# Every second chunk of a gated recurrence mirrored, so that one product serves two chunks on a level, with four level buffers and another order of VectorE's and ScalarE's steps

## The reference

```
x += 0.5 * swiglu(rmsnorm(x))                      # D_FF = 2816
p  = rmsnorm(x) @ w_in ; q,f,i,g | B,C,u = split(p)
     f = lb + (1-lb)*sigmoid(f); k = 1-f           # 4 heads, state 128x128
     S_t = diag(f_t) S_(t-1) + k_t v_t^T ; o_t = S_t^T q_t
     o_hg = rmsnorm(o) * silu(g) ; o_cv = rmsnorm(B * dwconv3(C*u))
x += concat(o_hg, o_cv) @ w_out
x += cross_attention(rmsnorm(x), rmsnorm(mem))     # 256 memory tokens
x += 0.5 * swiglu(rmsnorm(x)) ; return rmsnorm(x)
```

## Time and profile before

| | |
|---|---|
| median of three runs | 1117.04 us |
| the profiled execution | 1116.83 us |
| its span, first to last instruction | 1115.0 us |
| granted TensorE clock, mean over the span | 0.998 |
| TensorE busy | 1103.8 us, 99% of the span |
| VectorE, ScalarE, GpSimd busy | 631.6, 527.8, 439.2 us |

### The profile page before, as it was taken

The page is one execution under the profiler, slowest core; times in us unless marked ns, Lnnn a source line. Parts: engine busy times, 40 slices in busy tenths (PEclk is TensorE's granted clock), DMA queues, the critical chain, the costliest instruction groups (busy, mean ns, idle before and its releaser), DMA issues.

```text
span 1115.0 us, 17502 instructions
## 1 busy us (share of the span) xinstructions
PE 1103.8 (99%) x6434; PEld 971.7 (87%) x6434; DVE 631.6 (57%) x923; ACT 527.8 (47%) x735; POOL 439.2 (39%) x546
## 2 busy tenths in 40 slices
PE   9999999999999999999999999999999999999997
PEld 7889999988888888888888888888899999988886
DVE  7887777442222668888668123466977777430012
ACT  6555555542323555654466443354555555542231
POOL 0000000486665544434548883163000000485651
PEclk9999999999999999999999999999999999999999
DMA  7287675332333221222313442122676665333312
GB/s 240 78 226 185 181 198 169 114 113 95 113 97 110 76 77 57 76 76 76 112 58 127 161 166 76 39 76 75 179 200 179 173 193 169 115 113 99 109 57 76
DMA packets 49458, 136.89 MB, mean 123 GB/s; under 512 B 4736, under 2 KB 11008, under 8 KB 49280
## 3 DMA queue, kind: packets, MB, share of 16 engines
q1 hardware_dynamic: 43888, 118.90, 31.2%
q0 software_dynamic: 4320, 15.73, 8.5%
q10 hardware_dynamic: 1200, 1.57, 0.4%
HBM read 134.09 MB, written 2.10 MB: 122 GB/s over the span
## 4 chain that ended last, share of the span: by engine, by line
PE 53%; POOL 25%; issue 21%; DVE 0%; POOLq 0%; DMA 0%; ACT 0%; DVEq 0%; SPq 0%; ACTq 0%
POOL wl L438 25%; PE bank L1463 8%; PE bank L1465 8%; PE bank L1464 8%; PE bank L1567 4%; PE bank L1569 4%; PE bank L1568 4%; PE score L1567 3%; PE score L1569 3%; PE score L1568 3%; PE o_bank L1567 1%; PE o_bank L1569 1%; PE o_bank L1568 1%; PE bank L1524 1%; PE bank L1528 0%
## 5 line engine op out<-in xcount | busy, mean ns | idle before, releaser
L438 POOL TENSOR_TENSOR wl<-raw,wh 128x256 fp32r<-128x256 f32 x512 | 412.9, 840 | 325.5 <-ACT wh L472 281.2
L472 ACT ACTIVATE wh<-raw 128x1024 fp32r<-128x1024 f32 x120 | 126.0, 1054 | 148.6 <-PE bank L1465 146.4
L1463 PE MATMUL bank<-xh,wh 128*128 128x512 f32 x456 | 182.3, 400 | 0.0
L1465 PE MATMUL bank<-xh,wl 128*128 128x512 f32 x456 | 177.8, 390 | 0.0
L1464 PE MATMUL bank<-xl,wh 128*128 128x512 f32 x456 | 177.5, 389 | 0.0
L452 POOL DMA_DIRECT2D raw<-w_all x30 | 26.1, 869 | 325.1 <-DMA raw<-w_all 325.1
L1463 PE MATMUL bank<-zr,wh 128*128 128x512 f32 (+1 forms) x374 | 142.5, 381 | 0.0
L1465 PE MATMUL bank<-zr,wl 128*128 128x512 f32 (+1 forms) x374 | 141.6, 379 | 0.0
L1464 PE MATMUL bank<-zr,wh 128*128 128x512 f32 (+1 forms) x374 | 140.4, 375 | 0.0
L916 DVE SCALAR_TENSOR_TENSOR x<-bank,x 128x512 f32<-128x512 f32 (+1 forms) x31 | 21.3, 686 | 175.8 <-PE bank L1465 175.8
L1464 PEld LDWEIGHTS bank<-xl,wh 128*128 128x128 f32 x456 | 85.7, 188 | 18.7 <-issue 1.7
(11 more groups left out here) (304 smaller groups left out, 2582.0 us busy)
## 6 DMA issues: line engine op xcount, KB each, us to landing
raw<-w_all SPq DMA_DIRECT2D x200, 512.0 KB, 3.3
raw<-w_all POOLq DMA_DIRECT2D x30, 512.0 KB, 5.4
zf<-w_all SPq DMA_DIRECT2D x30, 256.0 KB, 4.6
x<-x_t SPq DMA_DIRECT2D x8, 256.0 KB, 6.4
out_t<-x SPq DMA_DIRECT2D x8, 256.0 KB, 2.4
raw<-w_all SPq DMA_DIRECT2D x6, 256.0 KB, 6.2
memf<-mem_t ACTq DMA_DIRECT2D x1, 1024.0 KB, 4.8
raw<-w_all ACTq DMA_DIRECT2D x2, 256.0 KB, 4.8
```

Source lines behind the costliest of these rows:

```text
L438: ins = nc.gpsimd.tensor_tensor(wl[:, slot, two], raw[:, slot, two], wh[:, slot, two].bitcast(f32), SUB)
L472: nc.scalar.activation(wh[:, slot, :], raw[:, slot, :], ACT.Copy).then_inc(hi_ready, 1)
L1463: nc.tensor.matmul(out_, a[0], b_[0], start=first, stop=False)
L1465: return nc.tensor.matmul(out_, a[1], b_[0], start=False, stop=last)
```

## The change

Of each pair of chunks the first is now stored mirrored in time. Its keys then lie in the half of a block where the second chunk has its queries, and the other way round. The keys of both fill one stationary tile of 128 columns, and the queries of both one moving tile of 128, so that a level takes two matmuls of 128 columns instead of four of 64. What comes out is one 128 x 128 tile for each pair, its lower triangle for one chunk and its upper for the other; it is collected in `tri` and laid out into `attn` once a head with a second predicated copy. The values of chunks 0 and 2 are mirrored by two matmuls with an exchange matrix (`turn_v`), and the masks for the mirrored chunks are made once, on VectorE under the first down projection (`make_masks`) and with two matmuls. What moves between the two orders of time (q, f, the norm) is written in two halves of 256. Levels rotate through four buffers; `lf` and `convC` get other places. On VectorE the differences of levels 0 and 1 now stand in step A, those of 2 and 3 in L0, and so on, and the factors of a level stand ahead of the differences in L1 and L2; factors of level 6 go to K. On ScalarE the exponentials go one step earlier.

```diff
 def differences(h, a):                       # VectorE
-    if a == 6 or a < 2:
-        if h:
-            dve.wait_ge(score_done, score_no(h - 1, 6 if a == 6 else 4 + a) + 1)
-    else:
-        dve.wait_ge(score_done, score_no(h, a - 2) + 1)
+    if a >= 4:
+        dve.wait_ge(score_done, score_no(h, a - 4) + 1)
+    elif h:
+        dve.wait_ge(score_done, score_no(h - 1, 3 if a == 3 else 4 + a) + 1)
...
 def take_scores(h, a):
-    V_.copy_predicated(at_, mk, sc).then_inc(score_read, 1)
+    V_.copy_predicated(tri[:, :, :], mk, sc).then_inc(score_read, 1)
...
+    V_.copy_predicated(attn[:, :, :].rearrange("p (g c) n -> p g c n", g=2), mk, both_ways)\
+        .then_inc(attn_ready, 1)
...
 def step(kind, h, a):
     if kind == "A":
-        link(V_.tensor_tensor_scan(b[:, :], restart[:, :], lf, 0.0, MULT, ADD))
+        link(V_.tensor_tensor_scan(b[:, :], restart[:, :], lf[:, :], 0.0, MULT, ADD))
-        if h == 0:
-            differences(h, 0)
-            differences(h, 1)
+        differences(h, 0)
+        differences(h, 1)
+    if kind == "L" and a == 0:
+        differences(h, 2)
+        differences(h, 3)
+        dve.wait_ge(k_ready, h + 1)
+        dve.wait_ge(silu_done, SN["q", h] + 1)
+        factors(h, 0)
+        factors(h, 1)
+    if kind == "L" and a == 1:
+        factors(h, 2)
+        factors(h, 3)
+        differences(h, 4)
+        differences(h, 5)
+        take_scores(h, 0)
+        take_scores(h, 1)
+    if kind == "L" and a == 2:
+        factors(h, 4)
+        factors(h, 5)
+        differences(h, 6)
+        V_.tensor_tensor(eb_kd, last.to_broadcast([128, 2, 2, 128]), b_in, SUB).then_inc(diff_ready, 1)
+        take_scores(h, 2)
+        take_scores(h, 3)
     if kind == "K":
+        factors(h, 6)
         take_scores(h, 4)
         take_scores(h, 5)
...
 def step(kind, h, a):                        # ScalarE
-    if kind == "L" and (h, a) != (0, 0):
-        decays(h, a)
+    if kind == "L":
+        if (h, a) != (0, 0) and a == 0:
+            decays(h, 0)
+        decays(h, a + 1)
...
 def step(kind, h, a):                        # TensorE
-    for t in range(TT):
-        last = nc.tensor.matmul(score_bank[s % 2][:, width * t:width * (t + 1)],
-                                lhs[:, 128 * t:128 * t + 128], rhs[:, t], start=True, stop=True)
+    for g in range(2):
+        last = nc.tensor.matmul(sc[:, 128 * g:128 * g + 128], keys_of(l, g), queries_of(l, g),
+                                start=True, stop=True)
...
+def queries_of(a, g):
+    m, first = LEVELS[a], X[:, XW * x_slot(a) + 256 * g:XW * x_slot(a) + 256 * g + 1]
+    return bass.AP(first.tensor, first.offset, [list(first.ap[0]), [2 * m, 64 // m], [256 + m, 2], [1, m]])
...
+def turn_v(t):
+    if t == 0:
+        pe.wait_ge(group_read, G_V + TT + 4)
+    else:
+        pe.wait_ge(v_ready, 1)
+    nc.tensor.matmul(o_bank[:, :], swap.bitcast(f32), V[:, t, :], start=True, stop=True).then_inc(v_turned, 1)
```

More of the change, by code:

```diff
@@ L40 @@
 MASK_COLS = 64 * len(LEVELS) + 128
+PAIR = 258
+XW = T + 128
 U_FFN1 = 0
@@ L917, in update_x, with make_masks @@
                                         op0=MULT, op1=ADD).then_inc(group_read, 1)
+            def make_masks():
+                same = masks[:, 64 * len(LEVELS):]
+                dve.wait_ge(hid_lo, FC)
+                V_.memset(upper, 0.0)
+                link(V_.memset(lower.bitcast(f32), 0.0))
+                V_.tensor_copy(mirrored(swap), same)
+                for a, m in enumerate(LEVELS):
+                    mk = masks[:, 64 * a:64 * a + 64].rearrange("p (n m) -> p n m", m=m)
+                    up_, lo_ = (t_[:, 128 * a:128 * a + 128].rearrange("p (n s m) -> p n s m", s=2, m=m)
+                                for t_ in (upper, lower))
+                    V_.tensor_copy(up_[:, :, 1, :], mk)
+                    lo_ = lo_[:, :, 0, :]
+                    (part, (sn, n), (sm, _)) = [list(d) for d in lo_.ap]
+                    ins = V_.tensor_copy(bass.AP(lo_.tensor, lo_.offset + sn * (n - 1) + sm * (m - 1),
+                                                 [part, [-sn, n], [-sm, m]]), mk)
+                ins.then_inc(masks_in, 1)
+                dve.wait_ge(masks_in, 1)
+                total = gbuf[:, 1, T - 128:]
+                link(V_.tensor_tensor(total, upper[:, 0:128], upper[:, 128:256], ADD))
+                for a in range(2, len(LEVELS)):
+                    link(V_.tensor_tensor(total, total, upper[:, 128 * a:128 * a + 128], ADD))
+                V_.tensor_copy(triangles[:, 1, :], total)
+                link(V_.tensor_tensor(total, total, same, ADD))
+                link(V_.tensor_scalar(triangles[:, 0, :], total, -1.0, 1.0, MULT, ADD))
             def ffn(norm, which):
@@ L1155, in ffn @@
                 if which == 0:
+                    make_masks()
                     with dve.Fori(0, KC // 4) as i:
@@ L1280, in step @@
+                    V_.tensor_tensor(kd, kd, f_of(h), MULT).then_inc(kd_ready, 1)
                 if kind == "Q":
@@ L1303, in step @@
                     dve.wait_ge(rms_ready, R["N", h] + 1)
-                    V_.tensor_tensor(onrm, o_bank[:, :], osq[:, :], MULT).then_inc(o_read, 1)
+                    for c in range(2):
+                        out_ = by_chunk(onrm)[:, :, c, :]
+                        last = V_.tensor_tensor(out_ if c else mirrored(out_), by_chunk(o_bank[:, :])[:, :, c, :],
+                                                by_chunk(osq[:, :])[:, :, c, :], MULT)
+                    last.then_inc(o_read, 1)
                     dve.wait_ge(o_read, h + 1)
```

225 lines of the change are left out of this document (141 added, 84 removed).

## The result

The changed kernel takes 1134.37 us (median of four runs, 1132.64 to 1135.59) against 1116.67 for the kernel before, run four times beside it: a ratio of 1.0153, interval 1.0134 to 1.0173. The forecast of 1123.2 had the sign and most places of the stalls; the loss is 17.7 us where it had 6.4.

What follows compares the result with a forecast made beforehand. TensorE bounds the kernel now, with VectorE nearly level and setting the end of the recurrence after the change. 2.9 + 3.45 = 6.35 us on the profiled 1116.83 gave 1123.2 us; 8-in-10 range 1108.5 to 1127.

Steps and rivals of the forecast that it cites:

- TensorE: what goes: Score levels on TensorE: 0.38 us saved for each of 28 levels, 10.6 us in all.
- The rival of 128 being as dear as four 64: Score matmuls: two of 128 columns cost as much as four of 64, nothing saved, 1124 to 1127; chance 0.02.
- The rival of the slowly read moving tile: Queries at m = 1 and 2: alternating columns double the records' cost, 3.7 us over 8 levels, 1125 to 1127; chance 0.05.
- What comes: Added TensorE work: 1.8 us for turning the values and 0.4 for mask matmuls, 2.2 us in sum.
- Hidden work: make_masks, 8.5 us under VectorE's 12.45 us wait at the first down product, and mixer-start clearings: no cost.
- A new wait, head 0: Before head 0's first scores: TensorE stalls 3.4 us for factors behind added differences; head 1's query moves by +2.9 us.
- The stretch to the last key product: Head 1's query to head 3's last key product: VectorE's chain grows from 115.1 to 119.6 us and sets the end.
- the three waits that were to go: VectorE's waits in that stretch for kd (1.9 us), X (1.4) and scores (0.3) vanish: -3.6 us.
- The norm's idleness: VectorE before onrm in three norms: 2.4 us idle each instead of 1.7 in all, +5.5 us.
- Behind that point TensorE's work is the same: After head 3's last key product: TensorE's work unchanged and VectorE has idle time, so no difference.
- 1.05 us of slack: Between the end of head 3's last key product and TensorE's use of it: 1.05 us, subtracted from the chain's growth.
- TensorE stays the bound: Recurrence: VectorE's idle time absorbs the additions, TensorE's waits stay under 5 us; 1109.1 us, from 1105.7 to 1114; chance 0.33.

Runs made afterwards that it cites:

- g2: e7 with take_scores of levels 0 to 3 also moved ahead of the differences in L1 and L2: 1111.71 us (0.9955 to the kernel before).
- f4: Changed kernel's mirroring and four buffers, with VectorE's and ScalarE's steps in the old order and the mask tables at SBUF's far end: 1118.00 us (1.0007).
- e7: e1 plus head 0-1-level factors ahead of the differences of levels 2 and 3 in L0, and g4's norm edit: 1114.90 us (0.9983).
- h2: Kernel before with four unused VectorE differences of 256 columns ahead of head 0's first factors, to make TensorE stall: 1123.81 us (1.0054).
- g4: e1 with the norm's table load, Ln and Exp ahead of the slot's decays on ScalarE: 1118.88 us (1.0023).
- e1: Changed kernel with only its two new mask tables, levels and triangles, moved to the far end of SBUF: 1128.01 us (1.0094).
- e2: Kernel before with an unused tensor of 1152 bytes a partition ahead of the hidden tiles: 1121.34 us (1.0041).
- f1: Kernel before with its seven small tensors at the far end of SBUF, so later tensors begin at a multiple of 2048 bytes: 1119.51 us (1.0024).

## Why the prediction was wrong

Two terms failed. TensorE's work outside the change was put at no difference, and it took 4.9 us more. And a stall was taken to cost its length, where the clock that fell behind it added to the price. Without the 4.9 us the time would still be 1129.5, above the range. In the order of the prediction:

**"TensorE: what goes": 10.6 us.** About right. The kernel before first, then the changed one; a pair of levels lasts from its start to that of the next product:

```profile
377.60 1.89 PE L1703 MATMUL score<-X 128*128 128x64 f32 x16
379.30 0.48 PE L1463 MATMUL bank<-wh,xh 128*128 128x512 f32 x1
```

```profile
392.48 1.06 PE L1832 MATMUL score<-X 128*128 128x128 f32 x8
393.29 0.48 PE L1589 MATMUL bank<-wh,xh 128*128 128x512 f32 x1
...
406.31 0.82 PE L1832 MATMUL score<-X 128*128 128x128 f32 x4
406.96 1.06 PE L1836 MATMUL score<-qf 128*128 128x128 f32 x8
407.86 0.60 PE L1847 MATMUL n_bank<-ident,both 128*128 128x128 f32 x4
```

1.70 became 0.81 for a pair, and 0.84 became 0.65 for level 6. With some 0.87 for the pair of levels 4 and 5 (0.83 where nothing delays it, in g2) that is 2.8 in a head and 11.4 us in four. As the kernels run, short delays inside the groups take some of it back: f4, e7 and g2 keep 8.2 to 8.8 us. The term did not decide the forecast, since the sum went by VectorE's chain. The rival of 128 being as dear as four 64 falls.

The rival of the slowly read moving tile was right in kind and small in size. The four records of level 6 (m = 1) take 0.65 us, the eight of the diagonal, of the same shape but with queries that lie side by side, 0.90. The single records start 112 ns apart for m of 4 and more, 120 to 124 for m = 2 and 165 for m = 1; the keys are read side by side at every level. In the kernel before, all levels have 112. That is 0.2 us a head for level 6 and 0.04 for level 5, 1.0 us in all, where the rival had 3.7. What comes was right (0.85 for turning the values, 405.46 to 406.31).

**"Hidden work": nothing.** Right, but barely. `make_masks` took from 235.52 to 248.15, 12.6 us where I had 8.5, since its conversions of 64 columns from uint8 took 0.75 each while GpSimd worked and 0.18 without it. What is left of the 12.45 us of wait:

```profile
248.50 0.69 DVE L986 SCALAR_TENSOR_TENSOR x<-bank,x 128x512 f32 x1 [0.34 <-DVE triangles L1013]
```

**"A new wait, head 0": +2.9 with a stall of 3.4.** The last factor was forecast for 381.8; it ends at 383.51, and 2.4 of that came from ahead of the mixer. The stall is 1.66 and 1.02. So the mechanism is right and the size nearly (2.7 us for 3.4), and the step failed at its price: a stall was taken to cost its length. The stretch lost 5.2 us. From the first product behind the scores to the next scores it is 8.04 us (384.44 to 392.48) and was 5.56 (379.30 to 384.86): twelve products begun at half the clock, 2.5 us. h2, where nothing else is changed, loses 5.6 us at such a stall, of which 2.7 are the clock's.

**"The stretch to the last key product": 119.6 us, +4.5.** In the prediction's marks (414.86, where head 1's query is read, to 537.20, the end of the key product) it is 122.3 us, 2.7 too many; the table's marks give +7.0. VectorE is busy 99.6 us instead of 97.0, the 2.6 that the copy and the halves were put at, and the three waits that were to go are gone. The norm's idleness is 8.4 us instead of 1.7, so +6.7 where I had +5.5; by head 2.5 to 3.0. It is also the term that g4 takes away. The second predicated copy cost 0.80 us, as its row said:

```profile
L1346 DVE COPY_PREDICATED attn<-triangles,tri 128x512 f32<-128x512 uint8 x4 | 3.2, 802 | 0.1
```

The other 1.5 us fall to VectorE's own waits for TensorE, which the chain did not have: 3.2 us behind the first query in place of 1.1, most of it in one place.

```profile
DVE gb L1430 <- PE bank L1591: 2.0, 1, 2.0
```

So VectorE's chain was not alone in setting the end here. The stalls stand mostly where the prediction put them: before the first scores of heads 1 and 3 (1.6 and 1.9 us, where it had 1.5 and 4) and before the last level; at head 2 it is 0.3 and not 1.7. That half of them are waits for a score bank, because takes stand behind the differences, I had not seen; g2 is that fact used.

**"Behind that point TensorE's work is the same": 0.** This is the step that failed outright, together with the same assumption for all that lies ahead of the mixer. The instructions are the same, their operands' addresses are not. It is +2.4 ahead and +2.5 behind, and e1 and e2 show that the place of the tensors is the cause. In addition the 1.05 us of slack that I took off were not had: TensorE came out of the last stall at the lower clock (536.61 to 538.31 for eight matmuls of 128 columns that take 0.90 at 406.96) and lost 1.0 more.

**In sum.** 17.7 us = 6.4 of forecast + 4.9 of placement + 6.4 in the recurrence. By the table these last are 2.3, 2.5 and 2.1 (0.4 more, since the table is of one profiled run and its forecasts are rounded). The rows give 2.3 in head 0 and about 1 behind the last stall to the lower clock, 1.2 to the norm, about 1.5 to VectorE's waits for TensorE, and 1.05 to the slack that was not there. How much of the middle stretch the lower clock cost is not shown. The rival *TensorE stays the bound* was wrong for this order: 12.9 us of waits instead of under 5. With the order of g2 it comes nearer: g2 has no stall in head 0, so its figure is the rival's 1105.7, and 1111.7 were measured, with 4.4 us of waits left.

## What to carry to other kernels

When an allocation grows, compare the distance between starts of products far away from the change, before any cause is sought near it. A stall of TensorE of some 2 us in a dense stretch has two prices: its length, and here up to twice that where the granted clock fell behind it, which it did in 15 of 26 cases. A forecast should give both, and the new trace says which it was. And where two engines are level, the gain on one is worth only what the other's order lets through: here the same instructions gave 1128.0 or 1111.7 by their order alone.

## What was not expected of the hardware

- The distance of matmuls depends on where the tensor of the moving tile begins. With the place given modulo 256 (the period itself is not shown): for 512 columns 226.7 ns at 0 and 128, 233.3 at 64, 228.9 at 192; for 256 columns 120.0 at 0 and 128, 117.5 at 64 and 192. The latter are means over a mix of products, in which the weights too were partly in these tiles; in the kernel before, those that read none of them are some 119 apart, and in f1 all are 120.0. So whether it is the moving tile's place or that of both together stays open. Granted clock 1.00 throughout.
- The records of float32 matmuls (two for each matmul) of 128 columns start 112 ns apart when the moving tile's columns lie side by side or in runs of 4 and more, 120 to 124 in runs of 2, and 165 when each column stands alone (level 6). In the kernel before, those of 64 columns start 112 ns apart as well, also at level 6.
- A single wait of 1.66 us and one of 1.02 us behind it were followed by some 6 us at the lower of the two clocks, and by half of that in e1 and g4; h2 made some 6 us out of 1.71 and 0.33. Where g2 has waits of 1.1 us and less, the granted clock is 1.00 in every window of 5 us from 355 to 580, but so it is in e7 with a wait of 2.42.
- Conversions from uint8 of 64 columns: 0.75 us beside GpSimd's work, 0.18 alone. The Trainium skill, SBUF — State Buffer (SBUF: two separate sides), names two kinds of VectorE instructions that GpSimd locks out, those with two SBUF inputs and those in a two-port mode; these have one input, and no row here shows their mode.
